# Scatter of the expert rows in two halves, residual rows loaded early, and part of the last gating on GpSimd

## The chip, the cores and the metric

One core of one Trainium2 chip. The metric is the device time of one execution in microseconds; lower is better. The kernel before took 1703.68 us (median of three runs, 1699.58 to 1706.36).

## What is computed

One layer of a hybrid encoder for 1024 prompt tokens and 8 x 16 sample tokens (T = 1152 rows of D = 1024, float32): attention, then a mixture of experts, then a last RMS norm. The change touches the expert part and what follows it. Cut to what matters:

```
h2 = rmsnorm(x, g_moe) * (1 + scale2) + shift2
# 16 experts, two for each token
for e in range(16):
    act = silu(h2 @ w1[e]) * (h2 @ w3[e])
    moe = moe + combine[:, e] * (act @ w2[e])
x = x + gate2 * moe
y = rmsnorm(x, g_final)
```

The outputs are y and the new keys, values and forget gates of the two attention branches.

## The kernel before

The program is a row of stages, each a block with one instruction stream for each engine and semaphores between them, with a barrier of all engines at the end of each. The ones that matter here:

- The attention stage (`stage_items`, from line 850). On its side, SP writes zeros into the scratch tensor `moe_d` from the tile `blank`, nine row tiles and one spare, two in each of five of the 16 head steps (line 973).
- The tail stage (`stage_tail`, from line 1402) makes x1 (the residual after attention) and h2, writes both to HBM, routes the tokens, and sorts them into 33 slot tiles of 128 rows. Each slot tile belongs to one expert. GpSimd adds a shift row to h2 there (line 1497) and multiplies small tables (line 1508).
- The expert stage (`stage_experts`, from line 1732) runs over the 33 slot tiles. For tile n: GpSimd gathers 128 rows of h2 by token (`gather`, line 1798, four buffers); TensorE transposes them (line 1824); ScalarE and VectorE split rows and weights into a high and a low part (`high_up` 1879, `low_up` 1935, `high_rows` 1885, `low_rows` 1939, `high_down` 1897, `low_down` 1952); TensorE multiplies up (line 1836, three passes) and down (line 1857); ScalarE copies the left 512 columns of the result out of PSUM and VectorE the right 512 (`take`, lines 1909 and 1964) into one of two buffers `yo`; GpSimd adds the buffer to the rows of `moe_d` named by `dest` with an indirect, accumulating DMA (`add_rows`, line 1805). An `add_rows` waits for both halves of its tile and until the one before it has landed. A `take` waits until the `add_rows` of two tiles earlier has landed. SP loads the weights, 1 MB for each of w1, w3 and w2, into `plain` when the expert changes (lines 1341 and 1345), and between them the rows of the last stage: gate2 rows, g_final, and one of the nine tiles of x1 (`Last.load`, line 1317, `EARLY` = 1).
- The last stage (`stage_final`, from line 1985) runs over nine row tiles of 128 x 1024. SP loads tile t of `moe_d` (line 2004) and of x1 (line 2006). VectorE multiplies by gate2 (`total`, line 2027) and adds x1 (line 2030); ScalarE squares and sums (line 2017) and takes the root (line 2019); VectorE takes the reciprocal (line 2036) and scales (`norm`, line 2038); SP stores (line 2010). VectorE's order is written out by hand, so that the norm of a tile comes after the `total` of the next:

```
for t in range(TT + 1):
    if t < TT:
        total(t)
    if t >= 1:
        norm(t - 1)
```

The order of the GpSimd queue in the expert stage is also written out: after four gathers, step n issues gather n + 4 and then `add_rows` n - 2.

Of the kernel before, what the change touches and what calls it, by code (L numbers as in the profile page):

```python
# [29 lines left out]
EARLY = 1  # L30
# [23 lines left out]
def program(nc, x_prompt, x_sample, cache_sb_k, cache_sb_v, cache_fox_k, cache_fox_v, cache_fox_logf,  # L54
# [14 lines left out]
    moe_d = scratch("moe_d", (T + P, D))  # L69
# [21 lines left out]
    with top:  # L91
# [758 lines left out]
        def stage_items(yhi, ylo, first_q, first_in):  # L850

            ctx = ExitStack()
            with ctx:
# [19 lines left out]
                blank = sb("blank", [P, D])  # L873
# [61 lines left out]
                def _(sp):  # L935
# [6 lines left out]
                    for k, (f, h) in enumerate(heads):  # L942
# [355 lines left out]
        class Last:  # L1298


            def __init__(self):
                self.x1 = [sb(f"x1_{j}", [P, D]) for j in range(EARLY)]
                self.g2 = [sb(f"g2_{j}", [P, D]) for j in range(2)]
                self.gf = sb("gf", [P, D])
                self.x1_in = [sem(f"last_x1_in{j}") for j in range(EARLY)]
                self.g2_in, self.gf_in = sem("last_g2_in"), sem("last_gf_in")

            def load(self, sp, i):
# [6 lines left out]
                elif i < NB + 2 + EARLY:  # L1315
                    t = i - NB - 2
                    sp.dma_start(self.x1[t][:], x1_d[t * P:(t + 1) * P, :]).then_inc(self.x1_in[t], 16)
# [414 lines left out]
        def stage_experts(tile_expert, tile_side, tok, dest, share, first, last):  # L1732

            ctx = ExitStack()
            with ctx:
# [30 lines left out]
                def _(sp):  # L1766
# [17 lines left out]
                    for n in range(NT + 2):  # L1784
# [5 lines left out]
                        if n >= 16:  # L1790
                            last.load(sp, n - 16)

                @block.gpsimd
                def _(pool):
# [20 lines left out]
                    pool.wait_ge(y_out, 16 * NT)  # L1815
# [57 lines left out]
                def _(act):  # L1873
# [57 lines left out]
                def _(dve):  # L1931
# [28 lines left out]
                    def take(n):  # L1960
                        dve.wait_ge(down_done, 2 * n + 2)
                        if n >= 2:
                            dve.wait_ge(y_out, 16 * (n - 1))
                        dve.tensor_copy(yo[n % 2][:, 512:1024], G[:, 5, :]).then_inc(y_dve, 1)
# [20 lines left out]
        def stage_final(last):  # L1985

            ctx = ExitStack()
            with ctx:
                sb, sem = holder(ctx, "final")
                y = [sb(f"y{t}", [P, D]) for t in range(TT)]  # L1990
                x1 = last.x1 + [sb(f"x1{t}", [P, D]) for t in range(EARLY, TT)]
                g2, gf, g2_in, gf_in = last.g2, last.gf, last.g2_in, last.gf_in
# [3 lines left out]
                x1_in = last.x1_in + [sem(f"x1_in{t}") for t in range(EARLY, TT)]  # L1996
# [5 lines left out]
                def _(sp):  # L2002
                    for t in range(TT):
                        sp.dma_start(y[t][:], moe_d[t * P:(t + 1) * P, :]).then_inc(y_in[t], 16)
                        if t >= EARLY:
                            sp.dma_start(x1[t][:], x1_d[t * P:(t + 1) * P, :]).then_inc(x1_in[t], 16)
                    for t in range(TT):
                        sp.wait_ge(o_ready, t + 1)
                        dst = y_prompt[0, t * P:(t + 1) * P, :] if t < TT - 1 else y_sample.rearrange("b i n -> (b i) n")
                        sp.dma_start(dst, x1[t][:]).then_inc(o_out, 16)  # L2010
                    sp.wait_ge(o_out, 16 * TT)

                @block.scalar
                def _(act):
                    for t in range(TT):
                        act.wait_ge(x2_ready, t + 1)
                        act.activation(sqd[:], x1[t][:], ACT.Square, accum_out=ss[:, t:t + 1]).then_inc(squared, 1)  # L2017
# [88 lines left out]
```

## Time and profile before

| | us |
|---|---|
| median of three runs | 1703.68 |
| lowest, highest | 1699.58, 1706.36 |
| the profiled execution's own time | 1700.87 |
| its span in the trace | 1699.0 |
| TensorE busy in the span | 1510.4 (89%) |
| VectorE busy | 932.1 (55%) |
| ScalarE busy | 779.1 (46%) |
| GpSimd busy | 182.4 (11%) |

The profile is of one execution. Times in it are microseconds from the start of the span, unless marked ns. PE is TensorE, DVE is VectorE, ACT is ScalarE, POOL is GpSimd, SP is the engine that issues most DMAs; a q behind the name is the engine's sequencer. L1805 is line 1805 of the kernel. In the timelines a row is the start, the duration, the engine, the line, the operation with output and inputs, and in brackets how long the engine had been idle and what released it. A DMA queue's share is the time that its packets took, as a share of the 16 DMA engines' time in the stretch, and can pass 1. The granted clock is given in parts of TensorE's full speed.

### The profile page before, as it was taken

The numbers are of one execution on the slowest core, as the hardware profiler recorded it, in microseconds if no ns is written. First come the engines' busy times: TensorE is split into PE (matmuls) and PEld (weight loads), VectorE is DVE, ScalarE is ACT, GpSimd is POOL, SyncE is SP. The second block draws the span as 40 slices with busy tenths as digits, with TensorE's granted clock in tenths as the row PEclk, the third lists the DMA queues.
The fourth block names the chain that finished last, engine by engine and source line by source line (L and its number), as shares of the span: only waits on it lengthen the run. The fifth ranks groups of instructions, "written<-read, shape, count | busy, mean of one in ns | idle before, by whom it ended". The sixth has DMA issues, their size and how long they took to land. (4 is left out here: it accounts for less than half of the span.)

```text
span 1699.0 us, 23867 instructions
## 1 busy us (share of the span) xinstructions
PE 1510.4 (89%) x8837; PEld 1342.0 (79%) x8837; DVE 932.1 (55%) x1173; ACT 779.1 (46%) x1109; POOL 182.4 (11%) x131
## 2 busy tenths in 40 slices
PE   5499999999999997999999989979973998999950
PEld 3289889999999987999998979967862886888840
DVE  6622112222332427777777744543235997999947
ACT  8522111113233326777777741122112776787833
POOL 0000000000000002000000001112103333433320
PEclk9799999999999998999999989989976999999975
DMA  8235444446666658785746323444316799899538
GB/s 311 77 92 166 129 130 155 140 147 202 206 212 203 198 188 220 177 225 125 177 117 165 91 82 99 148 170 149 112 74 198 235 322 322 256 281 286 106 52 321
DMA packets 233077, 300.14 MB, mean 177 GB/s; under 512 B 86441, under 2 KB 171537, under 8 KB 232954
## 3 DMA queue, kind: packets, MB, share of 16 engines
q1 hardware_dynamic: 223458, 264.01, 51.0%
q0 software_dynamic: 9504, 34.61, 8.4%
q8 instruction: 71, 1.16, 0.3%
q14 instruction: 44, 0.36, 0.1%
HBM read 264.23 MB, written 87.81 MB: 207 GB/s over the span
## 5 line engine op out<-in xcount | busy, mean ns | idle before, releaser
L690 PE MATMUL G<-hhi,proj_whi 128*128 128x384 f32 x768 | 178.4, 340 | 0.0
L690 PE MATMUL G<-hhi,proj_wlo 128*128 128x384 f32 x768 | 176.0, 337 | 0.0
L690 PE MATMUL G<-hlo,proj_whi 128*128 128x384 f32 x768 | 176.0, 337 | 0.0
L1935 DVE TENSOR_TENSOR experts_ulo<-plain,experts_uhi 128x2048 fp32r<-128x2048 f32 x66 | 151.0, 2289 | 18.0 <-ACT experts_uhi L1879 11.3
L1039 PE MATMUL G<-items_WT,items_vt 128*128 128x128 f32 x1152 | 150.4, 276 | 0.5 <-ACT items_WT L1092 0.2
L1879 ACT ACTIVATE experts_uhi<-plain 128x2048 fp32r x66 | 126.6, 1920 | 33.8 <-PEq L80 23.4
L1039 PEld LDWEIGHTS G<-items_WT,items_vt 128*128 128x128 f32 x1152 | 139.1, 192 | 2.4 <-ACT items_WT L1092 2.0
L690 PEld LDWEIGHTS G<-hhi,proj_whi 128*128 128x128 f32 x768 | 135.9, 188 | 2.7 <-DVE proj_wlo L777 2.3
L690 PEld LDWEIGHTS G<-hhi,proj_wlo 128*128 128x128 f32 x768 | 137.7, 188 | 0.0
L690 PEld LDWEIGHTS G<-hlo,proj_whi 128*128 128x128 f32 x768 | 137.6, 188 | 0.0
L1836 PE MATMUL G<-experts_uhi,experts_ghi 128*128 128x512 f32 x264 | 108.9, 412 | 8.5 <-DVE experts_glo L1939 7.6
L1836 PE MATMUL G<-experts_ulo,experts_ghi 128*128 128x512 f32 x264 | 104.7, 397 | 0.0
L1836 PE MATMUL G<-experts_uhi,experts_glo 128*128 128x512 f32 x264 | 104.6, 396 | 0.0
L1092 ACT ACTIVATE items_WT<-TB 128x512 f32<-128x512 f32 (+3 forms) x208 | 94.1, 488 | 21.2 <-PE TB L1025 19.2
L777 DVE TENSOR_TENSOR proj_wlo<-proj_wraw,proj_whi 128x1024 fp32r<-128x1024 f32 x32 | 38.9, 1217 | 118.3 <-ACT proj_whi L712 118.3
L1132 DVE TENSOR_TENSOR_SCAN items_SC<-items_R,items_zer 128x256 f32<-128x256 f32 (+7 forms) x72 | 92.3, 1281 | 20.7 <-ACT items_R L1077 17.6
L1521 PE MATMUL G<-wide,mixhi 128*128 128x512 f32 x288 | 93.6, 407 | 9.9 <-DVE wide L1597 9.9
L1805 POOL DMA_INDIRECT moe_d<-experts_yo,all_dest x33 | 81.0, 2455 | 198.6 <-DMA moe_d<-experts_yo,all_dest 137.1
L1025 PE MATMUL TB<-all_ident,items_S 128*128 128x128 f32 x608 | 92.2, 276 | 8.4 <-DVE items_S L1136 8.0
L833 DVE SCALAR_TENSOR_TENSOR proj_olo<-G,proj_ohi 128x1152 fp32r<-128x1152 f32 x16 | 21.7, 1358 | 122.0 <-ACT proj_ohi L757 122.0
L1025 PEld LDWEIGHTS TB<-all_ident,items_S 128*128 128x128 f32 x608 | 69.5, 140 | 12.6 <-DVE items_S L1136 9.6
L712 ACT ACTIVATE proj_wvhi<-proj_wraw 128x1024 fp32r<-128x1024 f32 x40 | 42.1, 1058 | 79.8 <-DMA proj_wraw<-in_w_ada_dram 63.0
(306 smaller groups left out, 3179.4 us busy)
## 6 DMA issues: line engine op xcount, KB each, us to landing
plain<-in_w_dram SPq DMA_DIRECT2D x132, 512.0 KB
plain<-in_w_dram SPq DMA_DIRECT2D x33, 1024.0 KB
proj_wraw<-in_w_ada_dram SPq DMA_DIRECT2D x32, 512.0 KB
proj_wraw<-in_w_in_dram SPq DMA_DIRECT2D x24, 512.0 KB
qkhi_d<-proj_ohi SPq DMA_DIRECT2D x16, 576.0 KB, 2.8
qklo_d<-proj_olo SPq DMA_DIRECT2D x16, 576.0 KB, 3.0
gate_d<-proj_full SPq DMA_DIRECT2D x16, 576.0 KB, 4.4
merge_sg<-gate_d SPq DMA_DIRECT2D x16, 576.0 KB
```

The costliest lines, as they stand in the source:

```text
L690: m = pe.matmul(G[:, g + c, 0:CH], w[r][:, k, :], a[:, k, c * CH:(c + 1) * CH], start=k == 0 and q == 0, stop=k == KD - 1 and q == 2)
L712: act.activation(hi, src, ACT.Copy).then_inc(w_hi, 1)
L777: dve.tensor_tensor(lo, src, hi.bitcast(F32), ALU.subtract).then_inc(w_lo, 1)
L1025: m = pe.transpose(TB[:, x % 2, (b % 4) * P:(b % 4 + 1) * P], S[n % (AHEAD + 1)][:, b * P:(b + 1) * P], ident[:])
L1039: m = pe.matmul(out, vt[f][:, b, :], w[:, b, :], start=b == 0, stop=b == nblocks(n) - 1)
L1092: act.activation(WT[n % 2][:, 4 * c:4 * c + nb, :].rearrange("p b n -> p (b n)"), TB[:, x % 2, 0:nb * P], ACT.Copy).then_inc(t_taken, 1)
L1132: dve.tensor_tensor_scan(SC[:, lo:SEQ][:, ::-1], R[o % 2][:, 0:w][:, ::-1], zer[:, 0:1].to_broadcast([P, w]), 1.0, ALU.mult, ALU.add).then ...
L1521: m = pe.matmul(G[:, 2 * (t % 2) + half, :], a[:, k, t * P:(t + 1) * P], w[:, k, half * 512:(half + 1) * 512], start=k == 0 and q == 0, st ...
L1805: pool.indirect_dma_start(moe_d, bass.IndirectOffsetOnAxis(ap=dest[:, n:n + 1], axis=0), yo[n % 2][:], None, compute_op=ALU.add).then_inc( ...
L1836: m = pe.matmul(up(n), a[j][:, k, :], w[j][:, k, :], start=k == 0 and q == 0, stop=k == KD - 1 and q == 2)
L1879: act.activation(half(uhi[j], c), raw_up(side[n], c), ACT.Copy).then_inc(u_hi, 1)
L1935: dve.tensor_tensor(half(ulo[j], c), raw_up(side[n], c), half(uhi[j], c).bitcast(F32), ALU.subtract).then_inc(u_lo, 1)
```

## The change

The scratch tensor `moe_d` becomes two tensors, one for each half of 512 columns. `add_rows` becomes two indirect DMAs, each with its own semaphore: the first waits for ScalarE's half alone, the second for VectorE's, and each for its own predecessor of the tile before. The `yo` buffers become three, and a `take` waits for the scatter of its own half, three tiles back. The zeros are written by twice as many DMAs of half the size. All nine x1 tiles are loaded by SP at the end of the expert stage, into the memory of the weights and of one gather buffer, as soon as the last up weights are split and the last rows are transposed; `stage_final` no longer loads x1. It loads each row tile of `moe_d` with two DMAs. The multiplication by gate2 of row tiles 1, 3, 5 and 7 moves from VectorE to GpSimd.

```diff
-    moe_d = scratch("moe_d", (T + P, D))
+    moe_d = [scratch(f"moe_d{c}", (T + P, 512)) for c in range(2)]
...
                             for t in (2 * k - 4, 2 * k - 3):
-                                sp.dma_start(moe_d[t * P:(t + 1) * P, :], blank[:]).then_inc(blank_out, 16)
-                    sp.wait_ge(blank_out, 16 * (TT + 1))
+                                for c in both:
+                                    sp.dma_start(moe_d[c][t * P:(t + 1) * P, :], blank[:]).then_inc(blank_out, 16)
+                    sp.wait_ge(blank_out, 16 * 2 * (TT + 1))
...
-            def __init__(self):
-                self.x1 = [sb(f"x1_{j}", [P, D]) for j in range(EARLY)]
+            def __init__(self, plain):
+                flat = plain[:].rearrange("p a k n -> p (a k n)")
+                self.x1 = [flat[:, t * D:(t + 1) * D] for t in list(range(TT - 1)) + [13]]
...
-                self.x1_in = [sem(f"last_x1_in{j}") for j in range(EARLY)]
+                self.x1_in = [sem(f"last_x1_in{t}") for t in range(TT)]
...
+            def load_x1(self, sp, t):
+                sp.dma_start(self.x1[t], x1_d[t * P:(t + 1) * P, :]).then_inc(self.x1_in[t], 16)
...
-                yo = [sb(f"yo{j}", [P, D]) for j in range(2)]
+                yo = [sb(f"yo{j}", [P, D]) for j in range(3)]
...
-                y_out = sem("ey_out")
+                y_out = [sem(f"ey_out{c}") for c in range(2)]
...
+                    sp.wait_ge(u_lo, 2 * NT)
+                    sp.wait_ge(g_turned, NT)
+                    for t in range(TT):
+                        last.load_x1(sp, t)
...
                     def add_rows(n):
-                        pool.wait_ge(y_act, n + 1)
-                        pool.wait_ge(y_dve, n + 1)
-                        if n:
-                            pool.wait_ge(y_out, 16 * n)
-                        pool.indirect_dma_start(moe_d, bass.IndirectOffsetOnAxis(ap=dest[:, n:n + 1], axis=0), yo[n % 2][:], None,
-                                                compute_op=ALU.add).then_inc(y_out, 16)
+                        for c, ready in enumerate((y_act, y_dve)):
+                            pool.wait_ge(ready, n + 1)
+                            if n:
+                                pool.wait_ge(y_out[c], 16 * n)
+                            pool.indirect_dma_start(moe_d[c], bass.IndirectOffsetOnAxis(ap=dest[:, n:n + 1], axis=0), yo[n % 3][:, c * 512:(c + 1) * 512], None,
+                                                    compute_op=ALU.add).then_inc(y_out[c], 16)
...
-                        if n >= 2:
-                            act.wait_ge(y_out, 16 * (n - 1))
-                        act.activation(yo[n % 2][:, 0:512], G[:, 4, :], ACT.Copy).then_inc(y_act, 1)
+                        if n >= 3:
+                            act.wait_ge(y_out[0], 16 * (n - 2))
+                        act.activation(yo[n % 3][:, 0:512], G[:, 4, :], ACT.Copy).then_inc(y_act, 1)
...
+                on_pool = (1, 3, 5, 7)
+                n_pool = [sum(1 for i in on_pool if i < t) for t in range(TT + 1)]
...
                     for t in range(TT):
-                        sp.dma_start(y[t][:], moe_d[t * P:(t + 1) * P, :]).then_inc(y_in[t], 16)
-                        if t >= EARLY:
-                            sp.dma_start(x1[t][:], x1_d[t * P:(t + 1) * P, :]).then_inc(x1_in[t], 16)
+                        for c in range(2):
+                            sp.dma_start(y[t][:, c * 512:(c + 1) * 512], moe_d[c][t * P:(t + 1) * P, :]).then_inc(y_in[t], 16)
...
+                @block.gpsimd
+                def _(pool):
+                    pool.wait_ge(g2_in, 16 * (1 + NB))
+                    for t in on_pool:
+                        pool.wait_ge(y_in[t], 32)
+                        pool.tensor_tensor(y[t][:], y[t][:], g2[0][:], ALU.mult).then_inc(pool_gated, 1)
...
-                        dve.wait_ge(y_in[t], 16)
-                        dve.tensor_tensor(y[t][:], y[t][:], g2[t // (TT - 1)][:], ALU.mult).then_inc(gated, 1)
+                        if t in on_pool:
+                            dve.wait_ge(pool_gated, n_pool[t + 1])
+                        else:
+                            dve.wait_ge(y_in[t], 32)
+                            dve.tensor_tensor(y[t][:], y[t][:], g2[t // (TT - 1)][:], ALU.mult).then_inc(gated, 1)
+                            dve.wait_ge(gated, t + 1 - n_pool[t + 1])
                         dve.wait_ge(x1_in[t], 16)
-                        dve.wait_ge(gated, t + 1)
-                        dve.tensor_tensor(x1[t][:], x1[t][:], y[t][:], ALU.add).then_inc(x2_ready, 1)
+                        dve.tensor_tensor(x1[t], x1[t], y[t][:], ALU.add).then_inc(x2_ready, 1)
```

VectorE's `take` changes as ScalarE's does, with `y_out[1]`. In every other use a whole x1 tile is named `x1[t]` instead of `x1[t][:]`.

## Rows read from the trace of the kernel before

**Rows 1.** Waits, 1290 to 1656 us (who waited for whom: us, times, longest)

```profile
POOL moe_d L1805 <- DMA moe_d<-experts_yo,all_dest: 137.1, 23, 7.5
...
DVE experts_yo L1964 <- DMA moe_d<-experts_yo,all_dest: 5.6, 1, 5.6
```

**Rows 2.** Waits, 1394 to 1426 us alone

```profile
ACT experts_uhi L1879 <- DMA plain<-in_w_dram: 10.4, 5, 4.1
```

**Rows 3.** Busy time by stretch (us, PE, PEld, DVE, ACT, POOL, PEclk, DMA share, GB/s)

```profile
1500.00:1600.00 100.00, 99.13 (x478) 80.64 (x477) 99.12 (x84) 77.94 (x73) 37.15 (x20) 1.00 0.84 233
...
1398.00:1412.00 14.00, 12.89 (x64) 10.18 (x62) 9.53 (x8) 7.70 (x8) 4.30 (x4) 1.00 1.06 352
```

**Rows 4.** Timeline, the last expert tiles (start us, us, engine line op)

```profile
1609.37 9.69 SPq L1345 DMA_DIRECT2D plain<-in_w_dram  x2
...
1623.09 2.29 DVE L1935 TENSOR_TENSOR experts_ulo<-plain,experts_uhi 128x2048 fp32r<-128x2048 f32 x1
...
1627.04 2.89 POOL L1805 DMA_INDIRECT moe_d<-experts_yo,all_dest  x1 [6.83 <-DVE experts_yo L1964]
...
1635.10 1.85 POOL L1805 DMA_INDIRECT moe_d<-experts_yo,all_dest  x1 [5.16 <-DMA moe_d<-experts_yo,all_dest]
...
1638.56 0.60 ACT L1909 ACTIVATE experts_yo<-G 128x512 f32<-128x512 f32 x1 [5.80 <-PE G L1857]
...
1641.12 0.69 DVE L1964 COPY experts_yo<-G 128x512 f32<-128x512 f32 x1 [5.60 <-DMA moe_d<-experts_yo,all_dest]
...
1642.54 1.55 POOL L1805 DMA_INDIRECT moe_d<-experts_yo,all_dest  x1 [5.60 <-DVE experts_yo L1964]
...
1655.63 0.82 SPq L2004 DMA_DIRECT2D final_y<-moe_d  x2
```

**Rows 5.** Timeline of DVE in the final stage

```profile
1659.69 1.23 DVE L2027 TENSOR_TENSOR final_y<-final_y,all_g 128x1024 f32<-128x1024 f32 x1 [17.88 <-DMA final_y<-moe_d]
...
1666.55 1.22 DVE L2027 TENSOR_TENSOR final_y<-final_y,all_g 128x1024 f32<-128x1024 f32 x1
...
1667.87 1.23 DVE L2030 TENSOR_TENSOR final_x<-final_x,final_y 128x1024 f32<-128x1024 f32 x1
...
1670.40 1.22 DVE L2027 TENSOR_TENSOR final_y<-final_y,all_g 128x1024 f32<-128x1024 f32 x1
...
1693.98 1.28 DVE L2038 SCALAR_TENSOR_TENSOR final_x<-final_x,final_ss,all_gf 128x1024 f32<-128x1024 f32 x1
```

**Rows 6.** The scatters' line and their landing (ns min/median/max; first and last start us)

```profile
L1805 POOL DMA_INDIRECT moe_d<-experts_yo,all_dest x33: 1552/2850/3618, 1328.4 to 1642.5; - x33
...
DMA to landing us min/median/max: 6.2/8.8/11.1
```

**Rows 7.** The costliest DVE line of the expert stage

```profile
L1935 DVE TENSOR_TENSOR experts_ulo<-plain,experts_uhi x66: 2280/2290/2294, 1298.1 to 1623.1; 128x2048 fp32r<-128x2048 f32 x66
```

**Rows 8.** Timeline of POOL and DVE, 1150 to 1155 us

```profile
1151.18 2.34 POOL L1497 TENSOR_TENSOR tail_h<-tail_h,tail_mod 128x1024 f32<-128x1024 f32 x1 [26.35 <-DVE tail_h L1619]
...
1152.20 2.41 DVE L1611 TENSOR_TENSOR tail_x<-tail_x,tail_h 128x1024 f32<-128x1024 f32 x1
```

**Rows 9.** The same lines over the whole tail stage (ns min/median/max)

```profile
L1611 DVE TENSOR_TENSOR tail_x<-tail_x,tail_h x9: 1224/1225/2408, 1145.4 to 1251.9; 128x1024 f32<-128x1024 f32 x9
...
L1497 POOL TENSOR_TENSOR tail_h<-tail_h,tail_mod x8: 2342/2394/2398, 1151.2 to 1242.5; 128x1024 f32<-128x1024 f32 x8
```

**Rows 10.** A POOL line beside busy DVE (ns min/median/max)

```profile
L1508 POOL TENSOR_TENSOR tail_mod<-tail_mod,tail_wp x3: 1262/1712/3499, 1282.1 to 1285.0; 128x594 bf16<-128x594 bf16 x3
```

**Rows 11.** DMA queues, 1642.4 to 1649: one scatter alone (packets, MB, share)

```profile
q0 software_dynamic: 144, 0.52, 50.9%
```

**Rows 12.** DMA queues, 1664 to 1676: 4 KB packets

```profile
q1 hardware_dynamic: 1376, 5.03, 102.5%
```

**Rows 13.** DMA queues, 1404 to 1406: 1 KB packets of the weights

```profile
q1 hardware_dynamic: 571, 0.57, 89.3%
```

More of the change, by code:

```diff
@@ L29 @@
 MASKED = -1.0e30
-EARLY = 1
 LO = 32
@@ L872, in stage_items @@
                 zer = sb("zer", [P, 1])
-                blank = sb("blank", [P, D])
+                blank = sb("blank", [P, 512])
                 blank_out = sem("blank_out")
@@ L1814, in _ @@
                             add_rows(n - 2)
-                    pool.wait_ge(y_out, 16 * NT)
+                    for c in range(2):
+                        pool.wait_ge(y_out[c], 16 * NT)
                 @block.tensor
@@ L1961, in take @@
                         dve.wait_ge(down_done, 2 * n + 2)
-                        if n >= 2:
-                            dve.wait_ge(y_out, 16 * (n - 1))
-                        dve.tensor_copy(yo[n % 2][:, 512:1024], G[:, 5, :]).then_inc(y_dve, 1)
+                        if n >= 3:
+                            dve.wait_ge(y_out[1], 16 * (n - 2))
+                        dve.tensor_copy(yo[n % 3][:, 512:1024], G[:, 5, :]).then_inc(y_dve, 1)
                     side = Values(dve, tile_side, 1)
@@ L1990, in stage_final @@
                 y = [sb(f"y{t}", [P, D]) for t in range(TT)]
-                x1 = last.x1 + [sb(f"x1{t}", [P, D]) for t in range(EARLY, TT)]
-                g2, gf, g2_in, gf_in = last.g2, last.gf, last.g2_in, last.gf_in
+                x1, g2, gf, x1_in, g2_in, gf_in = last.x1, last.g2, last.gf, last.x1_in, last.g2_in, last.gf_in
                 sqd = sb("sqd", [P, D])
@@ L1995, in stage_final @@
                 y_in = [sem(f"y_in{t}") for t in range(TT)]
-                x1_in = last.x1_in + [sem(f"x1_in{t}") for t in range(EARLY, TT)]
+                on_pool = (1, 3, 5, 7)
+                n_pool = [sum(1 for i in on_pool if i < t) for t in range(TT + 1)]
+                pool_gated = sem("pool_gated")
                 gated, x2_ready, squared, rooted, inverted, o_ready, o_out = (
@@ L2003, in _ @@
                     for t in range(TT):
-                        sp.dma_start(y[t][:], moe_d[t * P:(t + 1) * P, :]).then_inc(y_in[t], 16)
-                        if t >= EARLY:
-                            sp.dma_start(x1[t][:], x1_d[t * P:(t + 1) * P, :]).then_inc(x1_in[t], 16)
+                        for c in range(2):
+                            sp.dma_start(y[t][:, c * 512:(c + 1) * 512], moe_d[c][t * P:(t + 1) * P, :]).then_inc(y_in[t], 16)
                     for t in range(TT):
@@ L2009, in _ @@
                         dst = y_prompt[0, t * P:(t + 1) * P, :] if t < TT - 1 else y_sample.rearrange("b i n -> (b i) n")
-                        sp.dma_start(dst, x1[t][:]).then_inc(o_out, 16)
+                        sp.dma_start(dst, x1[t]).then_inc(o_out, 16)
                     sp.wait_ge(o_out, 16 * TT)
+                @block.gpsimd
[4 more added lines that the diff above has]
+                        pool.tensor_tensor(y[t][:], y[t][:], g2[0][:], ALU.mult).then_inc(pool_gated, 1)
                 @block.scalar
@@ L2016, in _ @@
                         act.wait_ge(x2_ready, t + 1)
-                        act.activation(sqd[:], x1[t][:], ACT.Square, accum_out=ss[:, t:t + 1]).then_inc(squared, 1)
+                        act.activation(sqd[:], x1[t], ACT.Square, accum_out=ss[:, t:t + 1]).then_inc(squared, 1)
                         act.wait_ge(squared, t + 1)
@@ L2037, in norm @@
                         dve.wait_ge(inverted, t + 1)
-                        dve.scalar_tensor_tensor(x1[t][:], x1[t][:], ss[:, t:t + 1], gf[:], ALU.mult, ALU.mult).then_inc(o_ready, 1)
+                        dve.scalar_tensor_tensor(x1[t], x1[t], ss[:, t:t + 1], gf[:], ALU.mult, ALU.mult).then_inc(o_ready, 1)
                     for t in range(TT + 1):
@@ L2074, in program @@
                 stage_tail(mhi, mlo, oraw, tile_expert, tile_side, token, dest, share, whi, wlo, plain[:, 1], first)
-            last = Last()
+            last = Last(plain)
             stage_experts(tile_expert, tile_side, token, dest, share, first, last)
@@ L2078, in program @@
             nc.all_engine_barrier()
-        stage_final(last)
+            stage_final(last)
 _INS = ['x_prompt', 'x_sample', 'cache_sb_k', 'cache_sb_v', 'cache_fox_k', 'cache_fox_v', 'cache_fox_logf', 'c_prompt', 'c_sample',
```

3 lines of the change are left out of this document (removed).

## The prediction

> **What bounds the kernel now.** First the stage table. In a middle stretch of the expert stage DVE and PE are both busy for 99 of 100 us [rows 3]: a slot tile takes what DVE and PE need for it, about 9.7 us. The waits of the stage come next [rows 1]. POOL waits 137.1 us for its own scatters to land, the largest number there, but nobody waits for POOL: the only row in which another engine waits for a scatter is VectorE's last `take`, 5.6 us, and its end stands at 1641.12 [rows 4], six us after the scatter it needs had landed (the scatter at 1635.10 was released by that landing). What it waited for was PE's last product. The scatters are slow and hidden. What does reach the tiles is the weights: ScalarE waits five times for them, 10.4 us in all, and all five lie between 1394 and 1426 [rows 2], where experts of a single tile follow one another. There the DMA queues are full, share 1.06, and DVE is busy for 9.53 of 14 us [rows 3].
>
> Then the end. The last up weights are split by 1625.4 (1623.09 + 2.29), the halves of the last tile leave PSUM at 1639.16 (ScalarE) and 1641.81 (VectorE), the last scatter is issued at 1642.54, and it lands 6.2 us later, at 1648.7 [rows 4, 6]. The barriers follow, and SP starts the last stage at 1655.63. The first product on VectorE starts at 1659.69 and the last norm ends at 1695.26 [rows 5]: 35.6 us in which VectorE is bound, with a period of 3.85 us for a row tile (1666.55 to 1670.40). The chain of waits from 1655.6 to the end of the span is almost only VectorE.
>
> The profiled execution took 1700.87 us, 2.8 below the median of 1703.68. I sum against the first and carry the difference over to the median.
>
> **Part by part.**
>
> *Zeros.* Ten DMAs of 512 KB become twenty of 256 KB on SP, two more in each of five head steps. SP waits in those steps for the scores of a whole head, which take longer than its list, so this costs nothing; if the cover were gone, it would be some 0.4 us for each of the ten, by the 0.41 us for one issue in [rows 4] (0.82 for two).
>
> *Three `yo` buffers.* Nothing waits for a `yo` buffer [rows 1], so nothing is gained.
>
> *Two scatters for one: issue.* POOL takes 1.55 us for one where DVE idles and 2.85 in the median beside it [rows 6]. A tile has a gather and now two scatters: with some 1.3 us for the gather, up to 7.5 us with the gaps, within 9.7. Do the extra POOL instructions slow VectorE? Its costliest line takes 2280 to 2294 ns in all 66 cases, through 66 indirect DMAs on POOL [rows 7]: no. Behind the waiting scatter stands the gather of a tile four ahead, which has three tiles of slack. Cost nothing.
>
> *Two scatters for one: DMA time.* The same bytes go in twice the packets. A scatter alone took 0.509 x 6.6 = 3.36 us of all 16 engines, for 144 packets 0.37 us each [rows 11]. Plain 4 KB packets took 1.025 x 12 x 16 / 1376 = 0.143 us [rows 12] and 1 KB packets 0.893 x 2 x 16 / 571 = 0.050 us [rows 13], that is 0.031 for a KB and 0.019 for a packet. If a scatter behaves so, with its row read and the target read too, halving rows adds eight packets for an engine, twice 0.019 each: +0.3 us for a tile. If its time goes by the packet and not by the bytes, it is +3.36. The full stretch speaks for bytes: in 14 us 352 GB/s [rows 3] make 4.93 MB, 11.7 us at the 420 GB/s of [rows 12], and reading 2 x 0.52 MB of targets for two scatters makes 2.5 more: 14.2. I take +0.3, on the five tiles from 1378 to 1426 where the weights end last: **+1.5 us**, ends 0 and +16.8. The Trainium skill (Collectives: The Full Stack, "The bandwidth ceiling: the fold count and why AG != RS != AR") says that an add in a DMA is slow because it reads two sources. That is the reading by bytes, which I had from the stretch's sum.
>
> *The last scatter.* Its left half may go at ScalarE's 1639.16, before PE has finished. The right half goes when the whole one did, at 1642.54, with half the data. Data took 3.36 of the 6.2 us [rows 11, 6], so half saves 1.7. Against it stand the x1 loads.
>
> *x1 early.* SP has nothing left after its last weights at 1619 (1609.37 + 9.69) and starts nine loads at 1625.4, 4.7 MB, 11.2 us at 420 GB/s. They meet the scatters of 1627.04 and 1635.10, which ran alone. Those need 6.7 us of the engines, so all is through at about 1645, and the last right half loses perhaps 0.5 to its predecessor. Together **-1.2 us**. Lower end -2.5. Upper end: three scatters one behind the other at the stage's slowest 11.1 us and then 6.2 [rows 6], 1627.0 + 22.2 + 6.2 = 1655.4 for 1648.7: +6.7. In the last stage the x1 loads were beside VectorE's work, so their removal there gives nothing. The first row tile comes as two DMAs, the second issued 0.4 later, each with half to move: nothing either way.
>
> *Gating on GpSimd.* Taken off VectorE: four products, 1.32 us each from start to start of the next (1666.55 to 1667.87): -5.3 us. Put on POOL: an operation of this shape takes 2.39 us there [rows 9], four are 9.6, and the nine tiles last over 30, so it looks free. It isn't, by [rows 8]: POOL's TENSOR_TENSOR ran from 1151.18 to 1153.52; VectorE's, with two inputs in SBUF, was put down as starting at 1152.20 and took 2.41 instead of 1.23. It ended at 1154.61, 1.09 after POOL's. That is its own 1.23 less 0.14: it did all its work after POOL had ended. Eight others of this line, with no POOL operation beside them, took 1.22 [rows 9]. And it holds in the other direction: of three equal POOL operations one took 3.50 us and another 1.26 [rows 10], beside busy DVE. The two engines take turns. In the last stage every large operation of VectorE reads two SBUF tensors, and there is almost no idle time in which POOL could run. So each POOL product stops VectorE for 2.39 - 0.14 = 2.25 us: +9.0. Net **+3.7 us**; ends -5.3 (side by side) and +4.3 (4 x 2.39).
>
> Sum: +1.5 - 1.2 + 3.7 = **+4.0 us**: 1704.9 against the profiled execution, 1707.7 against the median. That is 0.23%, and 0.5% (8.5 us) is about what a measurement can tell from no change.
>
> **Rivals.**
>
> *Side by side* (0.12). POOL and VectorE don't block each other in the last stage, and VectorE's chain shortens by the full 5.3. For it: POOL's four products fit four times over into the stage. Against it: [rows 8, 9], though that is one case of this shape. Sum +1.5 - 1.2 - 5.3 = -5.0: 1698.7.
>
> *Packets, not bytes* (0.12): the other side. Place: the tiles from 1378 to 1426, where weights are already late. Price: 3.36 us for each of five pairs, +16.8, so 3.7 - 1.2 + 16.8 = +19.3: 1723.0. It decides from about 1.2 us for a pair (3.7 - 1.2 + 5 x 1.2 = 8.5), and beyond that more stretches fill, since the share is 0.84 even in the calm one [rows 3]. For it: 0.37 us for a 4 KB scatter packet against 0.14. Against it: the sum of the full stretch. Here a rule speaks against the change: the Trainium skill (DMA: Bandwidth & Descriptors, "Anatomy of one DMA - SWDGE (gpsimd) path") gives a GpSimd DMA 2.0 us fixed plus bytes / 436e3. By it a pair takes 5.2 us where one took 3.2; were this 2.0 engine time, the five tiles would cost +10 and the sum be 1716.2. No row here shows that it is engine time rather than delay.
>
> *x1 in the scatters' way* (0.10). The loads double the landing of the last scatters, and the upper end above comes true in part or whole: 3.7 + 6.7 + 1.5 = +11.9: 1715.6. For it: landing up to 11.1 where queues are full. Against it: 18 us of DMA work fit into 1627 to 1645.
>
> *Nothing but the buffers* (0.04). The split does not start the left half early, since POOL is still busy with the tile before, and the rest cancels: 1703.7 + 3.7 + 1.5 + 0 = 1708.9.
>
> **How the numbers follow.** The forecast has 0.62. Its own range is 1703 to 1712. With side by side (1698.7) and half of the x1 case the range is 1698 to 1716; outside lie most of the packet case and some of the x1 case. Faster by over 0.5% needs 1695.2, below even side by side; with its end term at -2.5 and no packet cost that is 1695.9: 0.05. Slower by over 0.5% (above 1712.2): the packet case 0.12, most of the x1 case 0.07, the upper edge of the forecast 0.03: 0.22. Within 0.5%: 0.73.
>
> **What would show it.** In the last stage's timeline: VectorE operations of 2.4 to 3.6 us instead of 1.23, each ending about 1.1 after a POOL product, and first product to last norm 39.3 us, not 35.6. Side by side would show 1.23 throughout and some 30.3. Early: ScalarE's waits for weights at 10 to 13 us in all, against over 20 in the packet case; the share of the software queue for a pair of scatters alone near 3.7 us, against 6.7. At the end: left half issued about 1640, right half near 1642.5 to 1643.5, SP's first load of the last stage about 1.2 earlier, relative to the last `take`. Wrong would be: no long VectorE operation at all; a `take` that waits for a scatter; a last landing more than 2 us later after the last `take` than the 6.9 of before (1641.81 to 1648.7).

## The result and the profile after

The changed kernel took 1710.04 us (median of 8 executions, 1708.37 to 1713.46) against 1702.99 us for the kernel before (median of 8, 1699.58 to 1706.36): ratio 1.0042, interval 1.0031 to 1.0052. That is 7.1 us slower, inside the predicted range and 2.3 us above the predicted time. The profiled execution took 1708.37 us, with a span of 1706.3. Beside the experiments below the kernel before was measured again, with medians of 1702.88, 1702.87 and 1702.54 us; a ratio given with them can differ in its last digits from that of the two medians.

The span cut at the same six marks in both traces (all starts and ends from the timelines, us):

| stretch | before | after | difference | forecast |
|---|---|---|---|---|
| start to ScalarE's first split of expert weights | 1295.17 | 1297.32 | +2.15 | 0 |
| from there to the end of VectorE's last `take` | 346.64 | 347.21 | +0.57 | +1.5 |
| from there to SP's first load of the last stage | 13.82 | 16.12 | +2.30 | -1.2 |
| from there to VectorE's first product | 4.06 | 3.82 | -0.24 | 0 |
| first product to the end of the last norm | 35.57 | 37.77 | +2.20 | +3.7 |
| the rest | 3.74 | 4.06 | +0.32 | 0 |

The first line is not the change. It is there already after the first stage, in a row that has nothing to do with it. Timeline of GpSimd, first 80 us, the changed kernel:

```profile
72.20 0.09 POOL L504 MEMSET proj_zero<- 8x1 f32 x1 [69.66 <-POOLq L79]
```

In the trace of before this row starts at 69.94. In the thirteen profiles taken here it lies between 69.16 and 73.75, between 69.16 and 72.78 with the two scatters and between 69.63 and 73.75 with the one, and two profiles of one and the same kernel have it at 69.86 and 72.78. From this row to the first line's end it is 1225.23 us before and 1225.12 after, and the doubled zeros lie in this stretch: SP issues them in 13.4 us instead of 7.5, hidden.

The end of the expert stage, for [rows 4]. Timeline of the changed kernel:

```profile
1628.16 4.38 SPq L1310 DMA_DIRECT2D plain<-x_d  x9
1628.53 1.55 POOL L1810 DMA_INDIRECT moe_d<-experts_yo,all_dest  x1 [5.59 <-ACT experts_yo L1915]
1630.39 2.30 POOL L1810 DMA_INDIRECT moe_d<-experts_yo,all_dest  x1 [0.30 <-issue]
1638.05 1.62 POOL L1810 DMA_INDIRECT moe_d<-experts_yo,all_dest  x1 [5.36 <-DMA moe_d<-experts_yo,all_dest]
1640.71 1.55 POOL L1810 DMA_INDIRECT moe_d<-experts_yo,all_dest  x1 [1.04 <-DMA moe_d<-experts_yo,all_dest]
1641.28 0.60 ACT L1915 ACTIVATE experts_yo<-G 128x512 f32<-128x512 f32 x1 [5.80 <-PE G L1863]
1643.84 0.69 DVE L1970 COPY experts_yo<-G 128x512 f32<-128x512 f32 x1 [5.60 <-PE G L1863]
1646.74 1.55 POOL L1810 DMA_INDIRECT moe_d<-experts_yo,all_dest  x1 [4.48 <-DMA moe_d<-experts_yo,all_dest]
1648.60 1.55 POOL L1810 DMA_INDIRECT moe_d<-experts_yo,all_dest  x1 [0.30 <-issue]
1660.65 8.92 SPq L2012 DMA_DIRECT2D final_y<-moe_d  x18
```

The left half of the last tile was ready at 1641.88 (1641.28 + 0.60) and went out at 1646.74, when the left half of the tile before had landed, 8.7 us after its issue at 1638.05. The right half followed at 1648.60, 4.07 us after the last `take` had ended at 1644.53; in the kernel before it was 0.73. The two halves of the tile before that were slower still: 9.5 us from 1628.53 to 1638.05, and 10.3 from 1630.39 to 1640.71. In the kernel before, the whole scatter of this tile took 8.1 (1627.04 to 1635.10). What they waited for shows in the DMA queues of the changed kernel, first 1628 to 1634 us, then 1634 to 1640, then 1640 to 1646 (packets, MB, share of the 16 engines):

```profile
q1 hardware_dynamic: 423, 1.58, 75.5%
q0 software_dynamic: 1, 0.00, 0.2%
...
q1 hardware_dynamic: 377, 1.37, 60.0%
q0 software_dynamic: 287, 0.52, 47.1%
...
q1 hardware_dynamic: 493, 1.77, 74.2%
q0 software_dynamic: 188, 0.35, 31.8%
```

q1 are the x1 loads, q0 the scatters; a pair of halves has 288 packets. The pair issued at 1628.53 and 1630.39 moved one packet before 1634, while the loads ahead of it took 98.2% of the engines (1630 to 1634), and the other 287 from 1634 to 1640, the two queues side by side at about half each. The half issued at 1638.05 then moved none before 1642.5: from 1640 to that moment the loads alone have a share of 102.9%. So the left halves stood some 5 and 4.5 us before their first packets. In the kernel with the split alone, below, the half issued at 1637.31 has its first packets 2 us later. The loads end at about 1646.

The last stage, for [rows 5]. Timeline of the changed kernel, DVE and POOL:

```profile
1664.47 1.23 DVE L2043 TENSOR_TENSOR final_y<-final_y,all_g 128x1024 f32<-128x1024 f32 x1 [19.94 <-DMA final_y<-moe_d]
1665.73 1.23 DVE L2046 TENSOR_TENSOR plain<-plain,final_y 128x1024 f32<-128x1024 f32 x1
1666.69 2.48 POOL L2024 TENSOR_TENSOR final_y<-final_y,all_g 128x1024 f32<-128x1024 f32 x1 [16.53 <-DMA final_y<-moe_d]
1669.20 1.23 DVE L2046 TENSOR_TENSOR plain<-plain,final_y 128x1024 f32<-128x1024 f32 x1 [2.24 <-POOL final_y L2024]
1669.52 9.68 POOL L2024 TENSOR_TENSOR final_y<-final_y,all_g 128x1024 f32<-128x1024 f32 x3 [0.35 <-DMA final_y<-moe_d]
...
1670.53 3.18 DVE L2054 SCALAR_TENSOR_TENSOR plain<-plain,final_ss,all_gf 128x1024 f32<-128x1024 f32 x1
1673.64 3.35 DVE L2043 TENSOR_TENSOR final_y<-final_y,all_g 128x1024 f32<-128x1024 f32 x1
1677.03 3.24 DVE L2046 TENSOR_TENSOR plain<-plain,final_y 128x1024 f32<-128x1024 f32 x1
```

The first product of GpSimd (row tile 1) is waited for: VectorE stands 2.24 us. The next three run from 1669.52 to 1679.20, one behind the other at about 3.2 us each, and beside each of them one VectorE operation takes 3.2 to 3.4 us instead of 1.2 to 1.3. These end at 1673.71, 1676.99 and 1680.27; the last is 1.07 after the last product. Everything behind them is as short as before.

The middle of the expert stage, for [rows 1] and [rows 3]. Waits of the changed kernel, 1292 to 1662 us (us in total, times, longest):

```profile
POOL moe_d L1810 <- ACT experts_yo L1915: 108.7, 31, 7.6
...
POOL moe_d L1810 <- DMA moe_d<-experts_yo,all_dest: 34.5, 18, 5.4
...
ACT experts_uhi L1885 <- DMA plain<-in_w_dram: 10.0, 4, 3.3
...
ACT experts_dhi L1903 <- DMA plain<-in_w_dram: 2.7, 2, 2.0
```

GpSimd's waits for its own scatters fell from 137.1 to 34.5 us; it now waits for ScalarE's half instead, and no `take` waits for a scatter, as before. ScalarE's waits for up weights are 10.0 us, 10.4 before. Stages of the changed kernel in windows (us, busy time of PE, PEld, DVE, ACT and POOL, granted clock, DMA share, GB/s):

```profile
1398.00:1412.00 14.00, 12.37 (x59) 9.49 (x58) 10.94 (x9) 7.82 (x7) 6.79 (x5) 1.00 1.07 343
1500.00:1600.00 100.00, 98.80 (x475) 80.39 (x474) 98.59 (x85) 79.34 (x75) 51.06 (x30) 1.00 0.90 235
```

The calm stretch shows what the split costs in DMA time: share 0.90 for 0.84 at the same GB/s, 6 us of engine time in 100 for some ten tiles. A pair of half scatters alone, 1618 to 1628, changed kernel:

```profile
q0 software_dynamic: 288, 0.52, 43.6%
```

That is 4.4 us of all 16 engines; two other windows of 10 us with one pair in each give 4.1. One whole scatter took 3.36 [rows 11]. And the costliest VectorE line, for [rows 7], beside twice as many DMAs on GpSimd:

```profile
L1941 DVE TENSOR_TENSOR experts_ulo<-plain,experts_uhi x66: 2279/2287/2310, 1300.3 to 1625.8; 128x2048 fp32r<-128x2048 f32 x66
```

### The profile page after: what moved, and what is told of

Its sections match the earlier page's. It is cut to its first block and busy times, and to the rows that moved or that the text cites. A ratio compares the mean times of both kernels' runs of the same rounds, so it can differ in the third digit from the quotient of the medians.

```text
span 1706.3 us, 23951 instructions
## 1 busy us (share of the span) xinstructions
PE 1513.5 (89%) x8837; PEld 1344.3 (79%) x8837; DVE 933.4 (55%) x1169; ACT 779.0 (46%) x1109; POOL 248.0 (15%) x168
## 5 line engine op out<-in xcount | busy, mean ns | idle before, releaser
L1810 POOL DMA_INDIRECT moe_d<-experts_yo,all_dest x66 | 134.9, 2044 | 148.4 <-ACT experts_yo L1915 108.7
L1238 POOL TENSOR_TENSOR merge_sg<-merge_sg 128x1152 f32<-128x1152 f32 x8 | 21.8, 2722 | 444.4 <-DVE merge_sg L1272 444.4
```

Source lines behind the costliest of these rows:

```text
L1238: pool.tensor_tensor(a[:], a[:], b[:], ALU.add).then_inc(mix_ready, 1)
L1810: pool.indirect_dma_start(moe_d[c], bass.IndirectOffsetOnAxis(ap=dest[:, n:n + 1], axis=0), yo[n % 3][:, c * 512:(c + 1) * 512], None, com ...
```

## The experiments

The questions were three: which part makes up the lost end of the expert stage (the split or the early x1 loads), whether GpSimd and VectorE take turns and at what price, and what the split costs in the middle. The numbers compared are the stretches of the table above, since a single part moves the total by 0.1 to 0.3%. "End" is last `take` to SP's first load (13.82 before), "last stage" is first product to last norm (35.57 before).

### The split alone

Two half scatters and three `yo` buffers; one x1 tile early, as before; nothing gated on GpSimd. Against the changed kernel:

```diff
-                    for t in range(TT):
-                        last.load_x1(sp, t)
+                    last.load_x1(sp, 0)
...
-                on_pool = (1, 3, 5, 7)
+                on_pool = ()
...
+                        if t >= 1:
+                            last.load_x1(sp, t)
```

> The change with its two scatters and three buffers alone: x1 as before (tile 0 early, eight in the last stage), no product on GpSimd. In the changed kernel the last scatter landed 9.1 us after the last take, 6.9 before. Theory A (the x1 loads did that): here it lands 5.5 to 6.9 us after, and the time is -1 to +1 us against before (expert stage +0.6). Theory B (the two halves themselves did it, by queueing on POOL and behind their predecessors): landing 8.5 to 9.5 us after the take, time +2 to +4. Packets by count: weight waits over 15 us.

Measured: 1702.25 us, ratio 0.9992 (0.9982 to 1.0002). End 11.92, 1.9 shorter than before. Last stage 35.00. Timeline of POOL in this kernel, the last two tiles:

```profile
1637.31 1.55 POOL L1809 DMA_INDIRECT moe_d<-experts_yo,all_dest  x1 [3.06 <-ACT experts_yo L1914]
1639.17 2.06 POOL L1809 DMA_INDIRECT moe_d<-experts_yo,all_dest  x1 [0.30 <-issue]
1643.30 1.55 POOL L1809 DMA_INDIRECT moe_d<-experts_yo,all_dest  x1 [2.08 <-ACT experts_yo L1914]
1645.49 1.55 POOL L1809 DMA_INDIRECT moe_d<-experts_yo,all_dest  x1 [0.63 <-DVE experts_yo L1969]
```

Here the left half goes when ScalarE has it, and the right half 0.28 us after VectorE's `take`. So the split does at the end what it says, with only one x1 load beside it (this kernel issues x1 tile 0 after the last up weights are split, where the kernel before loads it earlier in the stage). The first of the two theories holds: the two halves alone don't lengthen the end.

### x1 early alone

The changed kernel with one whole scatter, two `yo` buffers and nothing on GpSimd:

```diff
-                        for c, ready in enumerate((y_act, y_dve)):
...
+                        pool.wait_ge(y_act, n + 1)
+                        pool.wait_ge(y_dve, n + 1)
+                        if n:
+                            pool.wait_ge(y_out, 16 * n)
...
-                on_pool = (1, 3, 5, 7)
+                on_pool = ()
```

> The early x1 loads alone: whole scatters, two buffers, no product on GpSimd. Theory A (the loads are in the scatters' way): the last landing moves from 6.9 to 8 to 10 us after the last take, time +1 to +3 us against before. Theory B: landing 6.9, time within 0.5 us of before. Nothing to gain in the last stage by either: first product to last norm stays 35.1 to 35.6 us.

Measured: 1706.73 us, ratio 1.002 (1.001 to 1.003). End 18.30, 4.5 longer than before; last stage 34.99. Timeline of POOL, the last three tiles:

```profile
1630.88 2.89 POOL L1809 DMA_INDIRECT moe_d<-experts_yo,all_dest  x1 [6.69 <-DVE experts_yo L1968]
1643.52 1.55 POOL L1809 DMA_INDIRECT moe_d<-experts_yo,all_dest  x1 [9.75 <-ACT experts_yo L1913]
1650.37 1.55 POOL L1809 DMA_INDIRECT moe_d<-experts_yo,all_dest  x1 [5.29 <-DMA moe_d<-experts_yo,all_dest]
```

The scatter at 1630.88 stands beside nine loads issued from 1629.25, and the next is issued 12.6 us after it, 8.1 in the kernel before (1627.04 to 1635.10). And the line's own view has a row that neither kernel had:

```profile
  ACT experts_yo L1913: 6.2, 1
```

ScalarE's `take` waited 6.2 us for a scatter. The longest landing in this view is 11.9 us, and 0.6 of the rest is that `take`. So the third buffer, worth nothing in the kernel before, is needed once the loads slow a scatter down. The harm was underrated in the expectation too: the last landing is about 11.4 us after the last `take`, where 8 to 10 was expected, and the median 3.9 us up instead of 1 to 3.

### GpSimd gating alone

Whole scatter, two buffers, x1 as before; the four products on GpSimd.

```diff
-                    for t in range(TT):
-                        last.load_x1(sp, t)
...
+                        sp.dma_start(y[t][:], moe_d[t * P:(t + 1) * P, :]).then_inc(y_in[t], 16)
+                        if t >= 1:
+                            sp.dma_start(x1[t], x1_d[t * P:(t + 1) * P, :]).then_inc(x1_in[t], 16)
```

> The four products on GpSimd alone. Turn-taking: VectorE operations of over 3 us in the last stage, first product to last norm 37 to 39.3 us for 35.6, time +2 to +4 us. Side by side: 30.3 us and time -5.

Measured: 1706.06 us, ratio 1.0015 (1.0004 to 1.0027). End 13.78, as before; last stage 37.88. The gating alone reproduces the last stage of the changed kernel (37.77), and nothing of its end. Both numbers are as expected for turn-taking.

### The changed kernel without GpSimd gating, and without the early x1

The first is the changed kernel with `on_pool = ()` and without GpSimd's block. The second:

```diff
-                    for t in range(TT):
-                        last.load_x1(sp, t)
+                    last.load_x1(sp, 0)
...
+                        if t >= 1:
+                            last.load_x1(sp, t)
```

> The changed kernel with the gating put back on VectorE (two scatters and early x1 stay). The single parts measured apart add up if they are independent: end of the expert stage -1.9 (two scatters) + 4.5 (x1) = +2.6 us, last stage 35.0 us. So +2 to +4 us against before, and last VectorE take to SP's first load about 16.2 us. If the parts are not independent (the halves make the loads harmless), take to load is under 14 us and the time within 1 us of before.

> The changed kernel with x1 loaded in the last stage again, but for tile 0 (two scatters and GpSimd's products stay). If the loads are in the scatters' way: take to first load 11.9 us, last stage 37 to 38, time 0 to +3 us against before, 4 us under the changed kernel. If not: 16 us and no gain on the changed kernel. The eight x1 loads now stand between the y loads: if these come late for GpSimd, the last stage is over 38.

Measured: without gating 1707.47 us, ratio 1.0027 (1.0013 to 1.004), end 16.79, last stage 35.00. With gating but x1 late 1703.48 us, ratio 1.0006 (0.9995 to 1.0016), end 13.06, last stage 38.02. On the path the early loads are the dearer part of the change: they make up 3.1 us of the end with gating (16.12 against 13.06) and 4.9 without (16.79 against 11.92), the gating 2.2 to 3.0 us of the last stage. Both kernels came a little worse than expected, 16.8 for 16.2 and 13.1 for 11.9 at the end. The second kernel's end is 1.1 above the split alone, for the same code there; its last right half was issued 1.39 after the `take`, not 0.28. An end varies so between executions: the five profiles with the whole scatter and x1 late have 13.70, 13.78, 13.82, 14.30 and 15.14, the three with the split and x1 late 11.92, 11.92 and 13.06. The means are 1.8 us apart and the two groups don't meet.

### The dose of early x1

The split, nothing on GpSimd, four x1 tiles early and five late (`range(4)`, and `if t >= 4` in the last stage).

> Two scatters, no product on GpSimd, and only x1 tiles 0 to 3 loaded early (2.1 MB instead of 4.7), the rest in the last stage. If the harm is the DMA queues' load while the last three scatters go: between one tile early (take to SP's first load 11.9 us) and nine (16.2), at 12.5 to 14; time -1 to +2 us against before.

Measured: 1701.09 us, ratio 0.999 (0.9974 to 1.0007), end 14.18, last stage 34.99. With the two neighbours: 1, 4 and 9 early tiles give an end of 11.9, 14.2 and 16.8 us. The end grows with the bytes put beside the scatters (14.18 is just above the 12.5 to 14 that was expected), and the last stage is 35.0 us with any number of them: VectorE sets it, and the loads never did.

### What a GpSimd operation costs VectorE

The kernel before (with the order of two waits as changed, see below) and, in the last stage, four GpSimd operations on tiles that nobody else writes meanwhile and whose result nobody reads. First products with two inputs, then copies with one:

```diff
+                @block.gpsimd
+                def _(pool):
...
+                    pool.wait_ge(x2_ready, 1)
+                    for t in range(4):
+                        if t:
+                            pool.wait_ge(pool_gated, t)
+                        pool.tensor_tensor(idle[:], g2[0][:], gf[:], ALU.mult).then_inc(pool_gated, 1)
```

In the second the last line is `pool.tensor_copy(idle[:], gf[:])`.

> The kernel before, with four products on GpSimd added in the last stage that write to a tile nobody reads (inputs gate2 row and g_final, after the first tile's sum). VectorE's work is unchanged and waits for none of them. Turn-taking: each stops VectorE for 2.0 to 2.3 us, so +8 to +9 us, and the stage is 43.6 to 44.6 us instead of 35.6. Side by side: 0.

> As the run with four products nobody reads, but each GpSimd operation is a copy with one input instead of a product with two. Theory C (an operation of GpSimd holds VectorE off for as long as it runs, whatever it reads): VectorE operations lengthened by GpSimd's own duration, some 1 us each, so +3 to +5 us. Theory D (only two-input operations of GpSimd hold VectorE off): no VectorE operation over 1.3 us, time as before.

Measured, products: 1707.97 us, ratio 1.0032 (1.002 to 1.0043), last stage 42.49. Timeline, POOL and DVE:

```profile
1663.67 13.00 POOL L2026 TENSOR_TENSOR final_idle<-all_g,all_gf 128x1024 f32<-128x1024 f32 x4 [18.41 <-DVE all_x L2048]
1664.66 3.25 DVE L2048 TENSOR_TENSOR final_x<-final_x,final_y 128x1024 f32<-128x1024 f32 x1
...
1668.01 3.18 DVE L2056 SCALAR_TENSOR_TENSOR all_x<-all_x,final_ss,all_gf 128x1024 f32<-128x1024 f32 x1
1671.12 3.35 DVE L2045 TENSOR_TENSOR final_y<-final_y,all_g 128x1024 f32<-128x1024 f32 x1
1674.51 3.25 DVE L2048 TENSOR_TENSOR final_x<-final_x,final_y 128x1024 f32<-128x1024 f32 x1
```

Measured, copies: 1703.6 us, ratio 1.0013 (1.0002 to 1.0025), last stage 37.26. Timeline:

```profile
1667.36 7.77 POOL L2026 COPY final_idle<-all_gf 128x1024 f32<-128x1024 f32 x4 [18.11 <-DVE all_x L2048]
1668.34 1.94 DVE L2048 TENSOR_TENSOR final_x<-final_x,final_y 128x1024 f32<-128x1024 f32 x1
...
1670.39 1.87 DVE L2056 SCALAR_TENSOR_TENSOR all_x<-all_x,final_ss,all_gf 128x1024 f32<-128x1024 f32 x1
1672.18 2.05 DVE L2045 TENSOR_TENSOR final_y<-final_y,all_g 128x1024 f32<-128x1024 f32 x1
1674.27 1.94 DVE L2048 TENSOR_TENSOR final_x<-final_x,final_y 128x1024 f32<-128x1024 f32 x1
```

VectorE waits for none of these operations, and the four VectorE operations beside them are lengthened all the same: by 2.02, 1.90, 2.13 and 2.02 us by a product, and by 0.71, 0.59, 0.83 and 0.71 by a copy. So it is neither the data nor a semaphore, and one input is enough. The two engines really alternate: the four products start 3.25 us apart, where one alone takes 2.39 [rows 9], and in each period stands one VectorE operation. The size was missed in both expectations: a last stage of 43.6 to 44.6 us was expected for the products, and a lengthening by about 1 us each, or none, for the copies. Against the 35.0 us that a kernel with this order of waits has (next section), the products cost 7.5 us and the copies 2.2, each some 0.6 less than its four lengthenings together.

### The order of two waits

All kernels without gating had a last stage of 35.0 us, where the kernel before has 35.57, with x1 loaded early or late. What they share is an exchange in the diff that the prediction had not costed: before the add, VectorE waits first for its own product and then for x1, where it was the other way round. The kernel before with that alone:

```diff
-                        dve.wait_ge(x1_in[t], 16)
                         dve.wait_ge(gated, t + 1)
+                        dve.wait_ge(x1_in[t], 16)
```

> The kernel before, with nothing but the order of VectorE's two waits ahead of the add of a row tile exchanged, as the change has it (first the product, then x1). If that order is what shortens the last stage where nothing is gated on GpSimd, the add starts 1.25 us after the product in all nine tiles instead of 1.32, the period of a row tile is 3.79 us instead of 3.85, and first product to last norm takes 35.0 us instead of 35.6. If it comes from elsewhere (the transfers, the place of x1 in memory), the steps stay 1.32 and 3.85 and the stage 35.6. Either way the time stays within what one look can tell from the kernel before.

Measured: last stage 35.01 us (one execution, 1701.49 us). Timeline of DVE, one product, its add and the next product:

```profile
1667.75 1.22 DVE L2027 TENSOR_TENSOR final_y<-final_y,all_g 128x1024 f32<-128x1024 f32 x1
1669.00 1.23 DVE L2030 TENSOR_TENSOR final_x<-final_x,final_y 128x1024 f32<-128x1024 f32 x1
...
1671.54 1.22 DVE L2027 TENSOR_TENSOR final_y<-final_y,all_g 128x1024 f32<-128x1024 f32 x1
```

1.25 us from product to add, 1.32 in [rows 5] (1666.55 to 1667.87), and a period of 3.79 for 3.85, as expected. The time of one execution says nothing at this size; the steps do, and all nine are 1.25 or 1.26. Nine times 0.07 is 0.6, of which 0.06 goes back in a longer wait for the first root.

### Two versions again

The split alone and the split with four early tiles, in more executions.

> The kernel of the split alone (two half-row scatters, three y buffers, one x1 tile loaded early as before, nothing gated on GpSimd), in more rounds. Its end of the expert stage is 1.9 us shorter than that of the kernel before in the one profile, and the stage itself 1.2 us longer. If both repeat, the net is -0.7 us or -0.04% (ratio 0.9996, 1702.2 us); if the longer stage was chance of the execution, -1.9 us (0.9989, 1701.0 us). The rival of the packet cost, some 1.0 us in each crowded tile beyond the forecast, would give +1.5 us or more (1.001).

> The split with four x1 tiles loaded early and the other five in the last stage, in more rounds. The one profile has its end of the expert stage 0.4 us longer than that of the kernel before, so on the path it should be level: ratio 1.000 to 1.0005. The earlier median below that of the split alone (0.999) was then chance. If early x1 tiles bring something in the last stage that the profile of one execution does not show, this kernel is again below the split alone, at 0.999.

Measured: the split alone 1700.6 us, ratio 0.9988 (0.9974 to 1.0002), end 11.92 again, last stage 35.01; with four early tiles 1701.48 us, ratio 0.9997 (0.9984 to 1.0011), end 14.12. The split alone is the best version found. Both measurements put it a tenth of a percent below the kernel before (-0.08% and -0.12%), and each interval reaches 1.0002. The traces show 2.4 us less at its end and in its last stage: 1.9 from the end, and 0.56 from the exchanged waits, which are no part of the split. The expert stage was 1.2 and 3.9 us longer in the same two profiles, inside the spread given below. So a gain of 1 to 2 us is what the parts suggest, and these executions don't prove it. The gain that four early tiles seemed to have in the first measurement did not come back.

## Why the prediction was right, and where it was not

**Direction and size.** 1707.7 was predicted, 1710.0 came. That the sum is so near is in part luck. On the path the end came 3.5 us worse than forecast, the last stage 1.5 and the middle 0.9 better, and these errors nearly cancel; and of the 7.1 us measured, the traces place only 4.3, or 4.9 with the middle.

**The failed step is the end of the stage:** "the last right half loses perhaps 0.5 to its predecessor. Together -1.2 us". It was +2.3 in the profile of the changed kernel and +3.0 in that without gating. The half scatter itself was rightly costed (-1.7 forecast, -1.9 measured in the split alone, twice, and -1.8 between the means of all profiles). The x1 loads were not: +0.5 forecast, +3.1 to +4.9 measured (16.12 and 16.79 against 11.92 to 13.06). The sum of the work was nearly right: it said that all is through at about 1645, and the loads ended at about 1646. Wrong was to charge that work once, at the last right half alone. The scatters are a chain: each half may only be issued when its predecessor has landed. Behind the queued loads the left halves stood 4.5 to 5 us before their first packets moved, and the links from 1628.53, 1630.39 and 1638.05 took 9.5, 10.3 and 8.7 us from issue to the issue that they released. So the left half of the last tile, ready at 1641.88, was issued at 1646.74 (the prediction says about 1640), and the right half behind it, 4.07 us after the `take`. The rival that named this, x1 in the scatters' way, put the end at up to +6.7 and was given 0.10. It came true in part, +2.3 to +3.0, on top of the rest of the forecast, and the mark that the prediction set for its error was met: last landing at 1653.6 (1648.60 + 5.0), 9.1 us after the last `take`, 2.2 more than the 6.9 of before.

**GpSimd gating: the mechanism stands, and its size was a little high.** The forecast was -5.3 for four products off VectorE and +9.0 for four turns. Of the four turns one was none: the first product was simply waited for, its input having come late, and that this wait is as long as a forecast turn is chance. Measured, with the steps of the changed kernel: 2.24 of standing and 1.90, 2.13 and 2.01 of lengthening make +8.3; four products at the new 1.25 from start to start make -5.0; the order of the waits -0.6; and 0.5 us for the first root, which VectorE waits for in the kernels without gating (0.43 in the kernel before), is covered. Together +2.2. The side-by-side rival, which would have given 30.3 us, is out, and by the copies not only for products. The Trainium skill (SBUF — State Buffer, "SBUF: two separate sides") states that VectorE with two SBUF inputs and a GpSimd operation that reads SBUF exclude each other, for the whole instruction of the one that starts first. The traces agree that they exclude each other, with the 2.0 and 0.7 us above.

**The scatter's DMA time.** 0.75 to 1.0 us for a pair and not 0.3, so packets cost more than I took from the plain queues, yet far from the 3.36 of the packets rival. On the path little of it shows: weight waits of 12.7 us (10.0 + 2.7) against 12.0, inside the 10 to 13 that was forecast, though the six other profiles with the split have 8.5 to 16.3. The stage is +0.57 long, and that can't be told from chance. Over all thirteen profiles it took 346.6, 346.8, 347.0, 347.3, 347.6 and 349.9 us with the whole scatter (mean 347.5) and 345.3, 347.2, 347.8, 347.9, 348.2, 350.6 and 351.1 with the split (mean 348.3). The same kernel, the split alone, has 347.8 and 350.6 among them. A granted clock of 0.95 in the stage's second part (1.00 is 2.4 GHz) goes with the three longest, but also with 347.0 and 347.3. So the +1.5 is neither shown nor refuted. The Trainium skill (DMA: Bandwidth & Descriptors, "Anatomy of one DMA — SWDGE (gpsimd) path") gives 2.0 us and bytes / 436e3; by it I estimate 3.2 us for a whole scatter and 2.6 for a half. The shortest landings here were 6.2 in the kernel before and 5.0 in the changed one (5.9 to 6.2 and 4.5 to 5.3 over all profiles), so most of the difference, and all of the rest, is more than the formula has. As engine time, which the prediction weighed with +10, its 2.0 us do not show: a second DMA in the pair added 0.75 to 1.0.

**Zeros, buffers, issue.** Nothing, as forecast. The waits' order was missed: it stood in the diff, at two lines that only seemed to move.

**What stays open.** The path accounts for +4.3 us (2.30 - 0.24 + 2.20) with +0.57 that may be chance, and the measured times say 7.1, by the interval 5.3 to 8.9. The changed kernel's ratio is what the parts give (1.0027 without gating and 1.0015 for gating alone), but the rest, 2.8 us by the median and 1.0 to 4.6 by the interval, has no place in the traces that repeats. The 2.15 us at the head of the profiled execution are not evidence for it, since they lie among the values of kernels with and without each part. The difference was followed in one profile for each kernel, and executions differ by several microseconds.

## What to carry to other kernels

Before moving loads into a stage's idle queues, look whether a chain of DMAs that wait for one another runs there: 4.7 MB that fit by bandwidth cost such a chain 3 to 5 us, in the one place where it was on the path, and hid nothing in return, because the stage they left was bound by VectorE. Before giving VectorE's work to GpSimd, look whether VectorE has idle time; where it had none, a 128x1024 product there cost 2.0 us and saved 1.25. And cost every line of a diff, the exchanged ones too.

## What was not expected of the hardware

- The order of two waits, one long fulfilled (x1) and one fulfilled as VectorE's own product ends, decides 0.07 us of VectorE's step: 1.32 us from product to add with the product's own semaphore waited for last, 1.25 with it waited for first.
- An unread GpSimd copy with one input lengthens a VectorE operation of two inputs by 0.7 us, a product by 2.0, and in turn GpSimd's product takes 3.2 us instead of 2.39.
- A scatter issued behind queued loads does not share the engines with them at first. A half issued at 1638.05 moved its first packet after 1642.5, while the loads held a share of 102.9%; without the loads one issued at 1637.31 moved its first after 1639. Why the wait is so long stays open.
- An accumulating scatter of 128 rows takes 3.4 us of all 16 engines in one piece and 4.1 to 4.4 in two halves with the same bytes. From one issue to the next it went from 8.1 us to 12.6 beside plain loads, 11.9 of them until it had landed.
